# Bias transfers of a neighbourhood attention: one half moved from the GpSimd queue to the sync engine's queue

## The reference

```python
bias = rpb_f[:, dr_idx, dc_idx].reshape(H, ncb, NA_QCB, nkey)
s_lat = einsum('bjqhd,bjkhd->bhjqk', q_b, k_s) * scale + bias      # 256 own tokens
s_ctx = einsum('bjqhd,bkhd->bhjqk', q_b, k_c) * scale              # 256 context tokens
p = softmax_f32(where(valid, concatenate([s_lat, s_ctx], -1), NEG_INF))
o = einsum(p[..., :nkey], v_s) + einsum(p[..., nkey:], v_c)
```

## Time and profile before

| | |
|---|---|
| Time before, median of 3 runs | 2737.92 us (2737.26 to 2740.18) |
| The profiled execution's own time | 2743.33 us |
| Its span | 2741.4 us |
| PE busy | 2639.1 us (96%) |
| DVE busy | 1197.7 us (44%) |
| ACT busy | 442.7 us (16%) |
| POOL busy | 108.2 us (4%) |
| Mean granted TensorE clock | 0.989 of full |

### The profile page before, as it was taken

The page is one execution under the profiler, slowest core; times in us unless marked ns, Lnnn a source line. Parts: engine busy times, 40 slices in busy tenths (PEclk is TensorE's granted clock), DMA queues, the critical chain, the costliest instruction groups (busy, mean ns, idle before and its releaser), DMA issues.

```text
span 2741.4 us, 48517 instructions
## 1 busy us (share of the span) xinstructions
PE 2639.1 (96%) x20537; PEld 1656.5 (60%) x20537; DVE 1197.7 (44%) x2895; ACT 442.7 (16%) x1054; POOL 108.2 (4%) x154
## 2 busy tenths in 40 slices
PE   8899999989899999999999998999979999999998
PEld 7659984865333233232332386699458967876993
DVE  3855675474110110110110166467655665344675
ACT  1231000133011010110110113200041001132000
POOL 1000000000100000000000011000000000050001
PEclk9999999999999999999999999999999999999999
DMA  7556555855999999999999946245504554232552
GB/s 224 175 182 206 169 170 183 269 167 197 338 418 419 417 416 411 410 419 406 408 420 410 413 153 108 70 154 170 172 14 154 170 172 135 77 85 70 169 170 93
DMA packets 234112, 642.91 MB, mean 235 GB/s; under 512 B 15673, under 2 KB 149185, under 8 KB 203056
## 3 DMA queue, kind: packets, MB, share of 16 engines
q1 hardware_dynamic: 225968, 616.89, 60.8%
q0 software_dynamic: 7264, 21.56, 3.5%
q10 hardware_dynamic: 672, 1.41, 0.1%
HBM read 626.73 MB, written 13.08 MB: 233 GB/s over the span
## 4 chain that ended last, share of the span: by engine, by line
PE 89%; DVE 6%; DMA 2%; issue 1%; POOL 1%; ACT 0%; DVEq 0%; ACTq 0%; POOLq 0%
PE pacc L1194 14%; PE pacc L1268 10%; PE pt L961 10%; PE pacc L1285 7%; PE pt L1268 7%; PE pt L1194 6%; PE pacc L1232 6%; PE pada L1294 4%; PE po L1268 3%; PE pacc L1135 3%; PE pt L1232 3%; PE pt L1173 2%; PE pt L1680 2%; PE pacc L1115 2%; PE po L1232 1%; DVE prob L2187 1%
## 5 line engine op out<-in xcount | busy, mean ns | idle before, releaser
L2527 DVE TENSOR_TENSOR gateb<-kT,pt 128x512 f32<-128x512 f32 (+1 forms) x32 | 19.9, 621 | 534.5 <-PE pt L1268 533.8
L1268 PE MATMUL pacc<-ring,bigc 128*32 128x512 f32 (+1 forms) x1920 | 188.3, 550 | 1.1 <-DVEq L2518 1.1
L961 PE MATMUL pt<-ring,hT 128*128 128x256 f32 x832 | 184.4, 381 | 0.0
L961 PEld LDWEIGHTS pt<-ring,hT 128*128 128x128 f32 x832 | 156.9, 190 | 25.6 <-issue 5.2
L1194 PE MATMUL pacc<-probT,prob 128*128 128x128 f32 x1440 | 170.6, 275 | 0.0
L1194 PEld LDWEIGHTS pacc<-probT,prob 128*128 128x128 f32 x1440 | 165.6, 192 | 0.0
L1285 PE MATMUL pacc<-ring,bigc 128*32 128x512 f32 x1280 | 151.2, 592 | 0.0
L1268 PE MATMUL pt<-ring,bigc 128*32 128x512 f32 (+1 forms) x1280 | 140.7, 560 | 8.2 <-DMA ring<-in_moe_w_up 8.2
L1232 PE MATMUL pacc<-prob,chunks 128*128 128x512 f32 x282 | 136.4, 592 | 0.0
L1268 PEld LDWEIGHTS pacc<-ring,bigc 128*32 128x32 f32 x1920 | 58.8, 110 | 127.2 <-issue 124.9
L2313 DVE TENSOR_TENSOR prob<-ring 128x512 f32<-128x512 f32 x86 | 59.5, 692 | 154.8 <-PE pacc L1194 108.5
(11 more groups left out here) (463 smaller groups left out, 4280.9 us busy)
## 6 DMA issues: line engine op xcount, KB each, us to landing
ring<-in_moe_w_down SPq DMA_DIRECT2D x80, 1024.0 KB, 17.5
ring<-in_w_gate_up SPq DMA_DIRECT2D x66, 1024.0 KB, 5.1
ring<-in_w_ada SPq DMA_DIRECT2D x48, 1024.0 KB, 5.3
ring<-in_moe_w_gate SPq DMA_DIRECT2D x48, 1024.0 KB, 8.5
ring<-in_moe_w_up SPq DMA_DIRECT2D x48, 1024.0 KB, 19.5
ring<-in_w_down SPq DMA_DIRECT2D x33, 1024.0 KB, 4.9
ring<-in_moe_w_gate SPq DMA_DIRECT2D x32, 768.0 KB, 15.0
ring<-in_moe_w_up SPq DMA_DIRECT2D x32, 768.0 KB, 12.8
```

The costliest lines, as they stand in the source:

```text
L961: ins = pe.matmul(t[:, q * 256:q * 256 + n], src[:, k, q * P:q * P + P], w[:, k, 0:n], start=(k == 0), stop=(k == KC - 1))
L1268: ins = pe.matmul(into[32 * j:32 * j + 32, 0:w].rearrange("p (t n) -> p t n", n=2 * 32), hcurv[:, kc, 32 * g:32 * g + 32], strip_columns(t ...
```

## The change

Batches 0 and 1 stay as they are. From batch 2 on, GpSimd issues only the transfers of the first 64 partitions. Those of the second 64 partitions are issued by SP. They stand in SP's program behind the second tile of the last feed-forward network and ahead of its third, each batch behind its own wait for `bias_used`. GpSimd's `mask_bias` waits for the landing of both parts. Two semaphores that served loads which are done by then are used again for SP's parts, and have new names.

```diff
+        def bias_transfer(queue, b, i, rr, loaded):
+            pitch = NDR * SKW
+            for j in range(4):
+                src = rows(skew, (b.heads[j] * GW) * pitch + (GROWS - 1 - 2 * b.qt - rr) * SKW + GW - 1,
+                           [[pitch - 1, GW], [SKW, GROWS], [1, GW]])
+                dst = biasb[64 * rr:64 * rr + 64, (i % 2) * 1024 + j * S:(i % 2) * 1024 + j * S + S]
+                queue.dma_start(dst.rearrange("p (r c) -> p r c", r=GROWS), src).then_inc(loaded, 16)
...
                 sp.dma_start(slot_view(n, kind), src).then_inc(tile_loaded[n % SLOTS], 16)
+                if n == ffn_plan[-1][0] + 1:
+                    for i, b in enumerate(na_batches()):
+                        if i >= 2:
+                            sp.wait_ge(bias_used, i - 1)
+                            bias_transfer(sp, b, i, 1, (context_or_even_bias, x_or_odd_bias)[i % 2])
...
             def mask_bias(i):
-                pool.wait_ge(bias_loaded[i % 2], 128 * (i // 2 + 1))
+                pool.wait_ge(bias_loaded[i % 2], 128 + 64 * (i // 2))
+                if i >= 2:
+                    pool.wait_ge((context_or_even_bias, x_or_odd_bias)[i % 2], 16 + 64 * (i // 2))
...
                 if i >= 2:
                     pool.wait_ge(bias_used, i - 1)
-                for rr in range(2):
-                    r = 2 * b.qt + rr
-                    for j in range(4):
-                        src = rows(skew, (b.heads[j] * GW) * pitch + (GROWS - 1 - r) * SKW + GW - 1,
-                                   [[pitch - 1, GW], [SKW, GROWS], [1, GW]])
-                        dst = biasb[64 * rr:64 * rr + 64, (i % 2) * 1024 + j * S:(i % 2) * 1024 + j * S + S]
-                        pool.dma_start(dst.rearrange("p (r c) -> p r c", r=GROWS), src)\
-                            .then_inc(bias_loaded[i % 2], 16)
+                for rr in range(2 if i < 2 else 1):
+                    bias_transfer(pool, b, i, rr, bias_loaded[i % 2])
                 mask_bias(i)
```

More of the change, by code:

```diff
@@ L347, in build @@
         wide_sum = sem("wide_sum")
-        xc_loaded = sem("xc_loaded")
-        x_loaded = sem("x_loaded")
+        context_or_even_bias = sem("context_or_even_bias")
+        x_or_odd_bias = sem("x_or_odd_bias")
         ident_loaded = sem("ident_loaded")
@@ L737, in load @@
                 if n == 1:
-                    sp.wait_ge(x_loaded, 16)
+                    sp.wait_ge(x_or_odd_bias, 16)
                     sp.wait_ge(rows_loaded, 16 * len(row_loads[0::2]))
@@ L778, in _ @@
                     sp.wait_ge(slot_free[6], 1 + NE * moe_uses[6])
-                    sp.dma_start(xcv, W["ctx_2"][0].rearrange("(t p) n -> p t n", p=P)).then_inc(xc_loaded, 16)
+                    sp.dma_start(xcv, W["ctx_2"][0].rearrange("(t p) n -> p t n", p=P)).then_inc(context_or_even_bias, 16)
                     after_moe += range(SLOTS)
@@ L843, in _ @@
             pool.wait_ge(rpb_moved, 32)
-            pitch = NDR * SKW
             def mask_bias(i):
-                pool.wait_ge(bias_loaded[i % 2], 128 * (i // 2 + 1))
+                pool.wait_ge(bias_loaded[i % 2], 128 + 64 * (i // 2))
+                if i >= 2:
+                    pool.wait_ge((context_or_even_bias, x_or_odd_bias)[i % 2], 16 + 64 * (i // 2))
                 bb = biasb[:, (i % 2) * 1024:(i % 2) * 1024 + 1024].rearrange("p (j k) -> p j k", j=4)
@@ L1758, in _ @@
             due = counter()
-            act.dma_start(xv, W["x"][0].rearrange("(t p) n -> p t n", p=P)).then_inc(x_loaded, 16)
+            act.dma_start(xv, W["x"][0].rearrange("(t p) n -> p t n", p=P)).then_inc(x_or_odd_bias, 16)
             act.dma_start(const[:, 0:P + 2 * STRIPS], W["shape_constants"][:, 0:P + 2 * STRIPS]).then_inc(ident_loaded, 16)
@@ L1922, in context_stats @@
                 def context_stats():
-                    act.wait_ge(xc_loaded, 16)
+                    act.wait_ge(context_or_even_bias, 16)
                     act.wait_ge(slot_free[9], 1 + NE * moe_uses[9])
@@ L1936, in experts @@
                 expert(NE - 1, context_stats)
-            act.wait_ge(x_loaded, 16)
+            act.wait_ge(x_or_odd_bias, 16)
             act.wait_ge(vector_setup, CLEARED)
```

## The result

| | before | after |
|---|---|---|
| Median | 2739.08 us (17 runs) | 2747.91 us (17 runs) |
| Ratio of the runs | | 1.0028 [1.0021, 1.0035] |
| Profiled execution, span | 2741.4 us | 2746.8 us |

The change made the kernel slower by 0.28%, some 7.7 us (5.8 to 9.6 by the interval; the two medians alone lie 8.8 us apart). The forecast was +4.0 us, to 2741.9 us, and no measurable change, with 2745.0 us as the upper end. The time came out 2.9 us above that end, and the slowing is clear of the noise. Of the 6.0 us above 2741.9, 1.2 us have nothing to do with the change: the median of the kernel before is 2739.08 us in its 17 runs, and the forecast stood on 2737.92 from three.

A forecast was written before the change was run, and what follows sets the result against it. PE, busy 96%, bounds the span; in the last attention GpSimd's 8.65 us bias round exceeds the 7.02 us round. +4.4 (batch 2) - 1.7 (batch 7) + 1.3 (clock) = +4.0 us: 2737.92 to 2741.9 us; 80% range 2737.5 to 2745.0.

The forecast's parts named there:

- What the change removes: GpSimd's round in the attention falls from 8.65 to about 6.25 us; ceiling of any gain 1.69 us, or 1.34.
- the last of the prediction's own signs of being wrong: At the program's end: an end that moves by another amount than the `shift` of batch 7.
- Batch 2 late: In the last attention, SP's transfers move behind the second feed-forward tile; the `shift` of batch 2 starts 4.4 us late.
- the 2442 that was named as a sign of being wrong: In the last attention: a `shift` of batch 2 before 2442 would show the prediction wrong; 2443.5 was forecast.
- The clock: At the scores of batch 3, a short half-clock stretch after PE's 5.2 us idle time costs +1.3 us; bounds 0 and 2.6.
- the rival: PE stays at half clock for 6.8 us after its idle time, costing 2.7 to 3.4 us instead of 1.3; chance 0.2.
- the objection to that rival: Part of the 6.8 us half-clock stretch could fall into PE's idle time, where it costs nothing.
- Batch 7: At the end of the last attention, batch 7 no longer waits for its bias: -1.7 us.
- the 0.35 us that the prediction set aside: Part of batch 7's 1.69 us loss that may not be the bias's; if it stays, the gain is 1.34 us.
- Transfers that pass the tile: SP's halves pass the second feed-forward tile or run beside it: batch 2 2.3 us late, 2738.5 to 2739.8 us; chance 0.2.
- A late start that is hidden: Batch 2's late start does not show, so all of the 1.7 us gain does: 2736.2 us; chance 0.05.
- Runs on SP that move more slowly, or wait for those of batch 3 behind them: SP's short bias runs in the last attention take another 1.3 us: +5.3 us, 2743.2 us; chance 0.1.

The follow-up runs named there:

- changed_padded: The changed kernel plus 24 spare transfers that GpSimd issues before the attention; ratio 1.0019 [1.0010, 1.0028] of the kernel before, +5.2 us.
- tile_gate: Against the kernel before: SP takes half the bias only from batch 3 on; batch 2's masking also waits for the second feed-forward tile; ratio 1.0030, +8.2 us.
- before_again: The kernel before, unchanged, run once more with a profile; no ratio given, sum from the profile +0.3 us.
- spare_on_sp: The kernel before plus 24 transfers on SP into an unread spare table, at the changed kernel's place and with its waits; ratio 1.0002, +0.5 us.
- before_padded: The kernel before plus 24 spare transfers on GpSimd; a single profiled execution without a ratio, last drain 5.64 us.
- the three padded kernels with an early batch 2: 24 spare GpSimd transfers added, with SP's bias ahead of the feed-forward tiles (two timings, -4.1 and -3.0 us) or half the bias left out (-0.8 us).

## Why the prediction was wrong

**The step that failed** is in "What the change removes": GpSimd's issues were counted only for its round in the attention ("Four of eight issues a batch ... This is the ceiling of any gain"), and the sum ended at the `shift` of batch 7, as if all behind it moved rigidly. It did not, and that is the last of the prediction's own signs of being wrong: the `shift` of batch 7 moved by 5.65 us and the end by 8.3, both against the `shift` of batch 0. With 24 transfers fewer GpSimd's last drain is 8.09 us instead of 2.37 and holds the end for 4.2 us. With that term the forecast of +4.0 would have been +8.2; the sum from the profiles is +8.3 and the measurement +7.7. That these agree so well is luck: the attention lost 1.65 us more than the forecast had it (0.8 for batch 2, 0.5 for the clock and 0.35 for batch 7, below), and 1.6 us that the prediction did not have came back behind the attention. No row before the change spoke of the drain, since one of 2.37 us lay hidden behind the stores. Without it, in changed_padded, the change costs 5.2 us by the runs and 4.0 by the sum.

**Batch 2 late** was the right mechanism at the right place, with the size forecast as 4.4 us and measured as 5.2. From the tile's issue to the `shift` it was to be 8.6 us (2434.9 to 2443.5) and was 9.34 (2432.04 to 2441.38): the tile landed after 5.5 us instead of 5.1, the four transfers took 1.5 us behind it instead of 1.3, and the two handovers some 0.1 more. SP's issue took 0.61 to 0.67 us, not 0.43, and that cost nothing: the fourth began at 2434.48, 3.1 us before the tile landed. The `shift` of batch 2 stands at 2441.38, before the 2442 that was named as a sign of being wrong, but only because this execution's attention began 2.9 us earlier; by the distances the batch is late.

The prediction had weighed two rules of the Trainium skill. The Trainium skill (DMA: Bandwidth & Descriptors, "Queues, rings and completion order") has an engine take the descriptors of one queue in ring order. The trace agrees: tile and bias land in the order of issue, 1.5 us apart. By the Trainium skill (the same page, "Issuing engines are not separate DMA queues") a second issuing engine saves only the time of the issues. The trace agrees here too: from one masking to the next GpSimd took 8.6 to 8.8 us before (batches 4 to 7) and takes 6.3 to 6.4 now, 2.3 to 2.4 us less, and four issues take 2.4 us.

**The clock** was forecast as +1.3 us. It took 1.79 us. The stretch at half clock was 6.8 us long, as the rival had it, and not of the short kind that the forecast took; but 3.1 us of it lay within the idle time, as the objection to that rival said. That 1.3 us came near is therefore in part luck. The rival's price, 2.7 to 3.4 us, did not come about, and what made the kernel slower beyond doubt was not in it. In tile_gate the longer round took 2.25 us.

**Batch 7** gave back 1.34 us, not 1.7: the round from batch 6 to 7 is 7.38 us in every kernel without the wait, so the 0.35 us that the prediction set aside are not the bias's. But the wait went with a second price. The four profiles of kernels in which batch 7 waits (before, before_again, spare_on_sp, before_padded) show one half-clock stretch more behind it, of 3.4 us; the fourteen others show none between the `shift` of batch 7 and the end of PE's work. The rows are busy times and granted clock as above, two in the kernel before, then the changed kernel at the same place, then spare_on_sp:

```profile
2531.70:2533.60 1.90, 0.02 (x1) 0.00 (x0) 1.81 (x6) 0.00 (x0) 0.00 (x0) 1.00 0.00 0
2534.10:2537.40 3.30, 3.30 (x18) 3.30 (x17) 3.12 (x6) 0.00 (x0) 0.00 (x0) 0.50 0.02 5
```

```profile
2536.30:2539.60 3.30, 3.21 (x28) 3.21 (x29) 3.00 (x5) 0.00 (x0) 0.00 (x0) 1.00 0.02 5
```

```profile
2470.80:2474.10 3.30, 3.30 (x7) 1.92 (x8) 1.29 (x3) 2.02 (x6) 0.00 (x0) 0.50 0.00 0
```

It costs 1.6 us (B is 265.4 with a short drain, 263.85 without the wait). So by the profiles the ceiling of the gain was 2.9 us and not 1.7, and the expectations above, which all count 1.3 us for it, are 1.6 us short. The runs of the three padded kernels with an early batch 2 (-4.1, -3.0 and -0.8 us) do not clearly tell 2.9 from 1.3.

Where the stretch lies says more of its cause. In spare_on_sp and before_padded it begins 4.4 and 4.7 us behind the `shift` of batch 7, directly behind the idle time of 2.0 and 2.3 us that the wait gives PE. In before and before_again it begins 58 us behind that `shift`, and there PE has just been idle again, for 1.90 us (the first row). All 18 profiles have this second idle time, and in the fourteen without the wait the clock stays full behind it, as in the changed kernel. So an idle time of 1.9 us is followed by a half-clock stretch in one execution and not in another, and the one at 2474 us need not reach to 2534. What decides it stays open, and that the missing wait is what removes the stretch is not shown; it rests on four profiles against fourteen.

**The other rivals.** Transfers that pass the tile: no. A late start that is hidden: no, it showed with 5.2 us. Runs on SP that move more slowly, or wait for those of batch 3 behind them: only by 0.2 us, since batch 2 was complete 1.5 us after the tile and not 1.3. Batch 3 was not late a second time, and no weight tile was, as forecast.

## What to carry to other kernels

A queue that looks idle can be held by a slot wait: look up when its next instruction in program order can leave, not only whether the queue is busy, and put short urgent transfers ahead of the large one. Follow each engine whose list of instructions changes to the very end of the program; the end is a place where all engines wait for the slowest. Where single executions scatter by more than the effect, distances between two fixed instructions in the profile tell kernels apart to 0.2 us.

## What the hardware showed that was not expected

GpSimd's last drain took from 2.37 to 8.41 us. It changed with the list of transfers that GpSimd had issued, in no steady way, and not with 24 memsets more; for one program it repeated to some 5 ns in different executions (8.087 to 8.090 us in seven profiles with 24 transfers fewer, and 2.370 to 2.373 in three with the list of the kernel before). It waits for more than GpSimd's last operation: in the changed kernel that was over at 2740.1 us, and the drain at 2746.6.

The version that is left as the best, SP's bias transfers ahead of the feed-forward tiles and GpSimd's transfers filled up to their old number, took 0.9985 [0.9975, 0.9995] and 0.9989 [0.9980, 0.9999] of the kernel before, 3 to 4 us faster.
